# Expert results weighted before they are stored and added to their tokens' rows in DRAM: a routed expert stage on one Trainium2 core

## The chip, the cores and the metric

The kernel runs on 1 core of one Trainium2 chip. The metric is device time in microseconds (us) of one execution; the figure before the change is the median of three runs. Engines are named as in the profile: PE (TensorE), PEld (its weight loads), DVE (VectorE), ACT (ScalarE), POOL (GpSimd), SP (SyncE, which here only issues transfers). "DMA engines" are the core's 16 transfer engines, which all queues share.

## The reference, cut to what matters

Two transformer-like blocks run over 512 tokens of 1024 features (`S`, `D`), all in float32. The change touches the end of the second block: a mixture of experts, the residual sum and the last norm.

```python
hn2 = _rmsnorm(h, norm2_g) * (1.0 + scale2) + shift2
h = h + gate2 * _hier_moe(hn2, ...)
return _rmsnorm(h, final_g)
```

`_hier_moe` picks for each token one group of four (`MOE_GROUPS`) and in it the two best of eight experts (`EXPERT_TOPK`), each with a weight. An expert is silu(x Wgate) * (x Wup), times Wdown, with a hidden width of 256. So the 32 experts share 1024 (token, expert) results, and a token has exactly two, both in one group. The weights of all 32 experts are 96 matrices of 1 MiB each.

## The kernel before, in words

**Stages.** The program is a row of blocks; all engines meet between two of them. The first block of the reference, and the mixers of the second, are split float32 products (L210 to L212). The stage that matters is `nsa_end` (L2858): output projections, router, and then, in the same block, the experts, whose instruction streams `moe` (L3197) returns as five functions. `combine` (L3489) follows as a block of its own. A further pass over the experts (`moe_rest`, L3594) runs only if an expert has more than 64 tokens; the profile has no instruction of it.

**Experts in pairs.** Pair `i` of 16 (`NP_`) has experts `2i` and `2i+1`. Each gets 64 slots (`SLOTS`), so that a pair fills 128 partitions. `spread_ids` (L3447, DVE, 8 instructions), `find_ids` (L3455, PE) and `place_ids` (L3462, DVE) work out for every slot of a pair which token it holds: `from_row` is the token's row (0 to 511), `to_row` its result's row (the token's first or second expert: row t or 512 + t of `results`). An empty slot has an index beyond the bounds, and its row is not moved.

**A pair's work.** POOL gathers the tokens' rows from `rows` in DRAM (`gather`, L3471). PE turns them (L3233), DVE and ACT apply gain and shift (L3369, L3344), PE multiplies with the gate and up weights (L3257), ACT takes the silu (L3327), DVE the product (L3378), PE turns it (L3275) and multiplies with the down weights (L3288); DVE multiplies by the row of `gate2` into `y` (L3404, `take`), and POOL scatters the rows of `y` into `results` (L3438). `y` has four places; nothing orders one scatter behind the other.

**Weights.** 48 steps (`STEPS`, L1372), each one kind of matrix for both experts of a pair, 2 MiB in two DMAs of SP (`issue_step`, L1455), stand in this order: gate 0, up 0, then gate i, up i, down i-1. They have 8 places (`PLACES`). Steps 0 to 7 are issued as their places come free before and during the routing; step n of the others waits until PE is done with step n - 8 (L3220).

**The token rows.** After the last projection PE turns x into rows (`turn`, L2948), ACT scales them by the tokens' norm factor (`keep`, L3025) and SP stores them, four DMAs of 512 KiB, between steps 6 and 7 (L2918 to L2923). POOL waits for all four and for the pair's indices before it gathers pair 0 (L3189).

**The end.** `results` was filled with finite numbers during the attention (L2689). In `moe`, PE turns x once more (`turn_x`, L3239) and ACT keeps it (L3335). DVE works out each token's two weights (`shares`, L3381). When all scatters have landed, SP loads the first tile's two sets of results (L3222 to L3224), the block ends, `combine` loads the other three (L3502), DVE makes `x + w0 * first + w1 * second` (L3522, L3524) and the norm (L3528 to L3532, with ACT's L3514 and L3516), and SP stores each tile (L3506).

The order of SP's queue around the routing, as the code has it:

```python
                sp.wait_ge(logits_done, 1)
                self.issue_step(sp, 6)
                for t in range(TB):
                    sp.wait_ge(kept, t + 1)
                    sp.dma_start(d["rows"][toks(t), :], self.h_tok[:, t, :]).then_inc(rows_stored, 16)
                self.issue_step(sp, 7)
                moe_sync(sp)
```

## Time and profile before

| what | us |
|---|---|
| median of 3 runs | 2683.36 |
| lowest and highest of them | 2681.14, 2684.74 |
| the profiled execution's own time | 2686.17 |
| its span in the trace | 2684.1 |

The profiled execution took 2.07 us more than its span, and 2.81 us more than the median. Times of trace rows are from the start of the span. The profile's first part gives busy time of each engine, its second the span in 40 slices with the granted TensorE clock and the DMA engines' busy share; then come queues, the chain of work that ended last, the costliest groups of instructions, and the DMA issues with the time to landing. Views of a stretch give the same for some microseconds. A DMA's row gives the time that the issue took on its engine, not the transfer's.

### The profile page before, as it was taken

The numbers are of one execution on the slowest core, as the hardware profiler recorded it, in microseconds if no ns is written. First come the engines' busy times: TensorE is split into PE (matmuls) and PEld (weight loads), VectorE is DVE, ScalarE is ACT, GpSimd is POOL, SyncE is SP. The second block draws the span as 40 slices with busy tenths as digits, with TensorE's granted clock in tenths as the row PEclk, the third lists the DMA queues.
The fourth block names the chain that finished last, engine by engine and source line by source line (L and its number), as shares of the span: only waits on it lengthen the run. The fifth ranks groups of instructions, "written<-read, shape, count | busy, mean of one in ns | idle before, by whom it ended". The sixth has DMA issues, their size and how long they took to land. (4 is left out here: it accounts for less than half of the span.)

```text
span 2684.1 us, 33667 instructions
## 1 busy us (share of the span) xinstructions
PE 2524.1 (94%) x13581; PEld 1987.0 (74%) x13581; DVE 1482.2 (55%) x2202; ACT 998.0 (37%) x1412; POOL 331.6 (12%) x187
## 2 busy tenths in 40 slices
PE   8999999999999999999999999998999798979874
PEld 6777788888887778888887887776778565856542
DVE  4564456544636536545545665675764886445313
ACT  4246533222333555322223333334522587321112
POOL 0000004531400000225522000001000000001110
PEclk9999999999999999999999999999998897989997
DMA  4221133443322211434442334444352001369996
GB/s 151 82 72 55 63 117 119 143 142 127 107 90 74 64 63 64 141 104 144 146 142 79 94 84 133 151 133 127 117 180 79 17 15 66 96 255 371 424 425 249
DMA packets 265027, 355.99 MB, mean 133 GB/s; under 512 B 33444, under 2 KB 238756, under 8 KB 252196
## 3 DMA queue, kind: packets, MB, share of 16 engines
q1 hardware_dynamic: 256452, 333.30, 36.7%
q0 software_dynamic: 8320, 20.46, 2.1%
q8 instruction: 110, 1.80, 0.3%
q14 instruction: 49, 0.40, 0.0%
q10 hardware_dynamic: 96, 0.02, 0.0%
HBM read 337.38 MB, written 24.19 MB: 135 GB/s over the span
## 5 line engine op out<-in xcount | busy, mean ns | idle before, releaser
L210 PE MATMUL ps<-h_hi,w_hi 128*128 128x512 f32 (+1 forms) x1736 | 697.8, 402 | 22.0 <-DVE room L879 4.4
L212 PE MATMUL ps<-h_hi,w_lo 128*128 128x512 f32 (+1 forms) x1736 | 680.0, 392 | 0.0
L211 PE MATMUL ps<-h_lo,w_hi 128*128 128x512 f32 (+1 forms) x1736 | 680.0, 392 | 0.0
L187 ACT ACTIVATE w_hi<-w_raw 128x2048 fp32r<-128x2048 f32 (+1 forms) x168 | 316.8, 1886 | 742.5 <-PE ps L212 728.2
L192 DVE TENSOR_TENSOR w_lo<-w_raw,w_hi 128x2048 fp32r<-128x2048 f32 (+1 forms) x168 | 396.8, 2362 | 173.1 <-ACT w_hi L187 173.0
L210 PEld LDWEIGHTS ps<-h_hi,w_hi 128*128 128x128 f32 (+1 forms) x1736 | 328.2, 189 | 102.3 <-issue 35.5
L212 PEld LDWEIGHTS ps<-h_hi,w_lo 128*128 128x128 f32 (+1 forms) x1736 | 327.7, 189 | 71.2
L211 PEld LDWEIGHTS ps<-h_lo,w_hi 128*128 128x128 f32 (+1 forms) x1736 | 328.3, 189 | 69.8 <-issue 4.1
L210 PE MATMUL ps<-merged_hi,w_hi 128*128 128x512 f32 x640 | 249.8, 390 | 0.0
L212 PE MATMUL ps<-merged_hi,w_lo 128*128 128x512 f32 x640 | 249.1, 389 | 0.0
L211 PE MATMUL ps<-merged_lo,w_hi 128*128 128x512 f32 x640 | 249.0, 389 | 0.0
L1343 POOL TENSOR_TENSOR room<-room,silu_c 128x2048 f32<-128x2048 f32 x24 | 119.9, 4995 | 939.5 <-DMA room<-in_w_ada 939.5
L1271 DVE TENSOR_TENSOR x<-x,ps 128x1024 f32<-128x1024 f32 x38 | 46.4, 1221 | 224.5 <-PE ps L212 224.5
L212 PEld LDWEIGHTS ps<-merged_hi,w_lo 128*128 128x128 f32 x640 | 120.1, 188 | 25.2
L211 PEld LDWEIGHTS ps<-merged_lo,w_hi 128*128 128x128 f32 x640 | 120.2, 188 | 24.8
L210 PEld LDWEIGHTS ps<-merged_hi,w_hi 128*128 128x128 f32 x640 | 120.2, 188 | 24.6
L1346 POOL TENSOR_TENSOR room<-room 128x1024 f32<-128x1024 f32 (+1 forms) x48 | 117.3, 2444 | 3.8
L1289 DVE TENSOR_TENSOR merged_lo<-room,merged_hi 128x1024 fp32r<-128x1024 f32 x32 | 116.3, 3633 | 0.0
L879 DVE SCALAR_TENSOR_TENSOR room<-ps,x_rs 128x512 f32<-128x512 f32 x58 | 40.1, 691 | 134.5 <-PE ps L212 127.6
L1285 DVE SCALAR_TENSOR_TENSOR room<-ps,room 128x1024 f32<-128x1024 f32 x32 | 39.2, 1224 | 73.5 <-PE ps L212 73.3
L2818 ACT ACTIVATE nsa_p<-nsa_p,nsa_mx 128x512 f32<-128x512 f32 (+3 forms) x128 | 70.8, 554 | 18.8 <-DVE nsa_mx L2769 17.2
L3327 ACT ACTIVATE moe_silu<-ps 128x256 f32<-128x256 f32 x16 | 6.1, 383 | 171.8 <-PE ps L3257 171.8
(488 smaller groups left out, 3553.1 us busy)
## 6 DMA issues: line engine op xcount, KB each, us to landing
w_raw<-in_w_in SPq DMA_DIRECT2D x268, 256.0 KB, 3.7
w_raw<-in_w_up SPq DMA_DIRECT2D x128, 256.0 KB, 3.5
w_raw<-in_w_down SPq DMA_DIRECT2D x128, 256.0 KB, 3.7
room<-in_w_ada SPq DMA_DIRECT2D x96, 256.0 KB, 6.0
expert_over_h<-in_w_exp_down SPq DMA_DIRECT2D x10, 1024.0 KB, 25.3
w_raw<-in_w_out SPq DMA_DIRECT2D x32, 256.0 KB, 3.4
ssd_e<-chunk_decays SPq DMA_DIRECT2D x32, 256.0 KB, 4.4
w_raw<-in_w_ssm_out SPq DMA_DIRECT2D x32, 256.0 KB, 3.6
```

Of the source, the lines that this page charges most:

```text
L187: act.activation(self.hi[:, q, :, 0:cols], raw[:, q, :, 0:cols], ACT.Copy).then_inc(self.hi_ready, 1)
L192: dve.tensor_tensor(self.lo[:, q, :, 0:cols], raw[:, q, :, 0:cols], self.hi[:, q, :, 0:cols].bitcast(F32), ALU.subtract).then_inc(self.lo_ ...
L210: pe.matmul(out, w[0], x[0], start=start, stop=False)
L211: pe.matmul(out, w[0], x[1], start=False, stop=False)
L212: return pe.matmul(out, w[1], x[0], start=False, stop=stop)
L879: dve.scalar_tensor_tensor(kept(t, c), bank(t, c), factor, x_rs[:], ALU.mult, ALU.mult).then_inc(taken0 if c == 0 and t != T_SWK else W.ev ...
L1271: dve.tensor_tensor(two(self.x, t), two(self.x, t), self.pst[:, q, 0:n, :], ALU.add).then_inc(W.evicted[q], 1)
L1285: dve.scalar_tensor_tensor(r[:, q], self.pst[:, q, 0:n, :], 0.0, rs.unsqueeze(1).to_broadcast([P, n, S]), ALU.max, ALU.mult).then_inc(W.ev ...
L1289: dve.tensor_tensor(two(u[1], t), r[:, q], two(u[0], t).bitcast(F32), ALU.subtract).then_inc(u_low, 1)
L1343: pool.tensor_tensor(w, w, c, ALU.mult).then_inc(ada_step, 1)
L1346: pool.tensor_tensor(w[:, 0:half], w[:, 0:half], w[:, half:2 * half], ALU.add).then_inc(ada_step, 1)
L2818: act.activation(p[:, i, e, 0:W], p[:, i, e, 0:W], ACT.Exp, bias=mx[:, i, e:e + 1], scale=-1.0, accum_out=den[:, i, e:e + 1]).then_inc(exp ...
```

## The change

Every result is multiplied by its token's weight when DVE takes it from PSUM (the third operand of `take`), so that a token's two results can simply be added. The scatter becomes an indirect DMA with `compute_op=ALU.add` into the token's own row of `results`, where x was stored beforehand. What it takes:

- **Pairs of two groups.** `expert_of(i, j)` pairs expert e of group 0 with expert e of group 1 (pairs 0 to 7), and of groups 2 and 3 (pairs 8 to 15). A token's experts lie in one group, so no token is twice in a pair.
- **Indices.** `place_ids` makes a third index, `add_row`: the token's row, or for an empty slot row 512 + p of partition p. All 128 rows of a pair are in bounds and are written. One more DVE instruction in front of `placed`, one behind it.
- **Adds one after the other.** POOL waits until scatter i - 1 has landed before it issues scatter i.
- **x in DRAM.** PE turns x a second time right behind the token rows (`turn(4)` to `turn(7)`), ACT copies it to `y` (`x_kept`), SP stores it to `results`, four DMAs of 512 KiB, once gathers 0 and 1 have landed. `take` of pairs 0 to 3 waits for these stores. The filling of `results` in the attention, `turn_x` and `take_x` are gone.
- **SP's order.** The token rows are stored ahead of step 6. Step 7 follows behind the stores of x.
- **Weights by slot.** `shares` moves from the sixth pair to the start; ACT stores the 2 x 512 weights (two DMAs from 128 partitions, 4 bytes a piece) to `d["shares"]` behind its first silu; POOL clears a small tile once and gathers, for each pair, 128 single weights by `to_row` (16 indirect DMAs more).
- **The wait for `passed`** moves from PE's first turn of `moe` to its first down product.
- **The end.** SP loads all four tiles of `results` in `moe` (four DMAs in place of eight in two blocks); `combine` has no adds, only the norm.

The diff, cut to what runs:


```diff
@@ -1389,6 +1389,11 @@
...
+def expert_of(i, j):
+
+    return (2 * (i // ME) + j) * ME + i % ME
+
...
@@ -1457,7 +1462,7 @@
...
+            w = self.d[("w_exp_gate_2", "w_exp_up_2", "w_exp_down_2")[kind]].rearrange("o e k n -> (o e) k n")[expert_of(i, e)]
...
@@ -2686,16 +2691,12 @@
...
-                for i in range(2):
-                    part = self.d["results"][i * S:(i + 1) * S, :].rearrange("(p r) n -> p (r n)", p=P)
-                    sp.dma_start(part, self.x[:].rearrange("p k s -> p (k s)")).then_inc(filled, 16)
...
-                sp.wait_ge(filled, 16 * 2)
...
@@ -2915,11 +2916,16 @@
                 W.done(sp, *wo[3])
                 for n in range(3, 6):
                     self.issue_step(sp, n)
-                sp.wait_ge(logits_done, 1)
-                self.issue_step(sp, 6)
                 for t in range(TB):
                     sp.wait_ge(kept, t + 1)
                     sp.dma_start(d["rows"][toks(t), :], self.h_tok[:, t, :]).then_inc(rows_stored, 16)
+                sp.wait_ge(logits_done, 1)
+                self.issue_step(sp, 6)
+                for i in range(2):
+                    sp.wait_ge(self.x_landed[i], 16)
+                for t in range(TB):
+                    sp.wait_ge(x_kept, t + 1)
+                    sp.dma_start(d["results"][toks(t), :], self.y[:, t]).then_inc(x_stored, 16)
                 self.issue_step(sp, 7)
                 moe_sync(sp)
 
@@ -2946,10 +2952,12 @@
...
-                    if t >= 2:
+                    if 2 <= t < TB + 2:
                         pe.wait_ge(kept, t - 1)
+                    elif t >= TB + 2:
+                        pe.wait_ge(x_kept, t - TB - 1)
                     for k in range(KC):
-                        mm = pe.transpose(turn_ps(t)[:, k * P:(k + 1) * P], self.x[:, k, toks(t)], self.c("ident"))
+                        mm = pe.transpose(turn_ps(t)[:, k * P:(k + 1) * P], self.x[:, k, toks(t % TB)], self.c("ident"))
...
@@ -3000,9 +3008,8 @@
...
-                for t in range(1, TB):
+                for t in range(1, 2 * TB):
                     turn(t)
-                pe.wait_ge(kept, TB)
...
@@ -3010,14 +3017,15 @@
...
+                pe.wait_ge(x_kept, TB)
...
+                pe.matmul(self.ps[:, 5, 0:1], self.c("ones"), over[:], start=True, stop=True).then_inc(over_sum, 1)
                 pe.wait_ge(gate_taken, 1)
-                pe.matmul(self.ps[:, 1, 0:1], self.c("ones"), over[:], start=True, stop=True).then_inc(over_sum, 1)
...
@@ -3064,6 +3072,9 @@
...
+                for t in range(TB):
+                    act.wait_ge(turned, TB + t + 1)
+                    act.activation(self.y[:, t], turn_ps(TB + t), ACT.Copy).then_inc(x_kept, 1)
...
@@ -3112,7 +3123,7 @@
...
+                link(dve.tensor_scalar(self.id_work[:, 4:5], self.c("token1")[:, 0:1], float(S - 1), None, ALU.add))
...
@@ -3221,7 +3233,8 @@
...
-            self.load_results(sp, 0, self.results_landed)
+            for t in range(TB):
+                sp.dma_start(self.first[:, t], d["results"][t * P:t * P + P, :]).then_inc(self.results_landed[t], 16)
...
@@ -3280,6 +3282,8 @@
...
+                else:
+                    pe.wait_ge(passed, 1)
...
-            pe.wait_ge(passed, 1)
...
@@ -3347,6 +3339,10 @@
...
+            act.wait_ge(shared, 1)
+            for i in range(2):
+                to = d["shares"][i * S:(i + 1) * S, :].rearrange("(t p) o -> p (t o)", p=P)
+                act.dma_start(to, self.place_w[:, i], allow_slow_non_contiguous=True).then_inc(shares_stored, 16)
...
@@ -3401,10 +3395,14 @@
...
-                dve.tensor_tensor(y[:, i % YR], y_ps, self.gate_row, ALU.mult).then_inc(y_ready, 1)
+                else:
+                    dve.wait_ge(x_stored, 16 * TB)
+                dve.wait_ge(self.share_landed[i % 4], self.shares_before + 16 * (i // 4 + 1))
+                dve.scalar_tensor_tensor(y[:, i % YR], y_ps, share[:, i:i + 1], self.gate_row, ALU.mult, ALU.mult).then_inc(y_ready, 1)
...
+            shares()
...
@@ -3429,14 +3425,27 @@
...
+            def gather_share(i):
+                pool.indirect_dma_start(share[:, i:i + 1], None, d["shares"], bass.IndirectOffsetOnAxis(ap=self.to_row[:, i:i + 1], axis=0),
+                                        bounds_check=2 * S - 1, oob_is_err=False).then_inc(self.share_landed[i % 4], 16)
+
+            pool.memset(share[:], 0.0).then_inc(share_cleared, 1)
             gather(2)
             gather(3)
+            pool.wait_ge(share_cleared, 1)
+            pool.wait_ge(shares_stored, 32)
+            for i in range(4):
+                gather_share(i)
             for i in range(NP_):
                 if i + 4 < NP_:
                     gather(i + 4)
                 pool.wait_ge(y_ready, i + 1)
-                pool.indirect_dma_start(d["results"], bass.IndirectOffsetOnAxis(ap=self.to_row[:, i:i + 1], axis=0), y[:, i % YR], None,
-                                        bounds_check=2 * S - 1, oob_is_err=False).then_inc(y_stored[i % YR], 16)
+                if i >= 1:
+                    pool.wait_ge(y_stored[(i - 1) % YR], 16 * ((i - 1) // YR + 1))
+                pool.indirect_dma_start(d["results"], bass.IndirectOffsetOnAxis(ap=self.add_row[:, i:i + 1], axis=0), y[:, i % YR], None,
+                                        bounds_check=2 * S - 1, oob_is_err=True, compute_op=ALU.add).then_inc(y_stored[i % YR], 16)
+                if i + 4 < NP_:
+                    gather_share(i + 4)
...
@@ -3460,23 +3469,19 @@
...
         link(dve.scalar_tensor_tensor(to, v, -1.0, none, ALU.add, ALU.add))
         dve.tensor_copy(self.to_row[:, i:i + 1], to)
         link(dve.tensor_scalar(back, to, float(S), -float(S), ALU.is_ge, ALU.mult))
-        dve.tensor_tensor(self.from_row[:, i:i + 1], to, back, ALU.add).then_inc(placed, 1)
+        link(dve.tensor_tensor(token, to, back, ALU.add))
+        dve.tensor_copy(self.from_row[:, i:i + 1], token).then_inc(placed, 1)
+        dve.tensor_tensor(self.add_row[:, i:i + 1], token, spare, ALU.min)
...
@@ -3490,17 +3495,14 @@
...
-                for t in range(1, TB):
-                    self.load_results(sp, t, landed)
...
-                    act.wait_ge(summed, t + 1)
+                    act.wait_ge(landed[t], 16)
...
-                def add(t):
-                    dve.wait_ge(landed[t], 32)
-                    dve.scalar_tensor_tensor(first[:, t], first[:, t], self.place_w[:, 0, t:t + 1], x_tok[:, t], ALU.mult, ALU.add).then_inc(weighted, 1)
-                    dve.wait_ge(weighted, t + 1)
-                    dve.scalar_tensor_tensor(first[:, t], second[:, t], self.place_w[:, 1, t:t + 1], first[:, t], ALU.mult, ALU.add).then_inc(summed, 1)
-
                 def norm(t):
...
-                add(0)
-                for t in range(1, TB):
-                    add(t)
-                    norm(t - 1)
-                norm(TB - 1)
+                for t in range(TB):
```

## Rows read from the trace of the kernel before

**Rows 1.** The page: span, then DMA share and rate in 40 slices.

```profile
span 2684.1 us, 33667 instructions
...
DMA  4221133443322211434442334444352001369996
```

**Rows 2.** Two stretches: PE, PEld, DVE, ACT, POOL busy, clock, DMA share, GB/s.

```profile
2406.00:2408.00 2.00, 0.00 (x0) 0.00 (x0) 0.45 (x2) 0.00 (x0) 0.09 (x1) 0.50 0.98 410
...
2410.00:2412.00 2.00, 0.00 (x0) 0.00 (x0) 0.00 (x0) 0.00 (x0) 0.35 (x1) 0.50 0.51 142
```

**Rows 3.** Stretches of the expert stage, the same columns.

```profile
2440.00:2500.00 60.00, 60.00 (x465) 36.83 (x466) 38.16 (x158) 11.36 (x30) 10.11 (x10) 1.00 1.01 422
2500.00:2560.00 60.00, 51.81 (x376) 29.81 (x372) 14.73 (x37) 9.08 (x24) 8.07 (x8) 0.97 1.01 424
2560.00:2620.00 60.00, 47.11 (x332) 26.52 (x334) 11.03 (x23) 7.80 (x21) 6.03 (x6) 0.97 1.01 425
...
2640.00:2645.00 5.00, 4.22 (x22) 1.46 (x21) 0.28 (x1) 1.02 (x1) 0.00 (x0) 1.00 0.38 162
```

**Rows 4.** Order of time around the routing: start, length, engine, line, idle before it.

```profile
2385.17 3.73 SPq L2922 DMA_DIRECT2D token_rows<-nsa_gate  x4
...
2388.94 2.14 SPq L1461 DMA_DIRECT2D expert_over_h<-in_w_exp_down  x2
...
2403.47 0.16 DVE L3469 TENSOR_TENSOR from_row<-id_work 128x1 int32<-128x1 f32 x1
...
2407.91 1.13 POOL L3472 DMA_INDIRECT nsa_gate<-token_rows,from_row  x1 [331.38 <-DMA token_rows<-nsa_gate]
...
2412.30 1.95 PE L3233 MATMUL ps<-const,nsa_gate 128*128 128x128 f32 x8 [7.83 <-DMA nsa_gate<-token_rows,from_row]
...
2415.88 5.74 PE L3257 MATMUL ps<-expert_first,moe_x 128*64 128x256 f32 x32 [1.64 <-issue]
...
2421.65 0.80 SPq L1461 DMA_DIRECT2D expert_first<-in_w_exp_gate  x2
...
2423.22 1.50 ACT L3344 ACTIVATE moe_x<-ps,par 128x128 f32<-128x128 f32 x4 [1.18 <-PE ps L3233]
...
2427.25 3.67 PE L3257 MATMUL ps<-expert_over_w,moe_x 128*64 128x256 f32 x32
```

**Rows 5.** DMA queues and issues, 2340 to 2684 us; last column: issue to landing.

```profile
q0 software_dynamic: 4608, 8.40, 6.5%
...
nsa_gate<-token_rows,from_row POOLq DMA_INDIRECT x16, 10.3
token_results<-results,to_row POOLq DMA_INDIRECT x16, 8.3
```

**Rows 6.** Order of time at the end of the stage.

```profile
2646.72 0.97 POOL L3438 DMA_INDIRECT token_results<-results,to_row  x1 [14.39 <-DVE results L3404]
...
2651.78 0.97 POOL L3438 DMA_INDIRECT token_results<-results,to_row  x1 [4.09 <-DVE results L3404]
...
2655.47 0.43 SPq L3479 DMA_DIRECT2D w_raw<-token_results  x1
2659.13 1.28 ACT L3511 ACT_TABLE_LOAD   x1 [7.31 <-PEq L2862]
...
2677.64 1.04 ACT L3514 ACTIVATE fin_sq<-expert_first 128x1024 f32<-128x1024 f32 x1
...
2677.97 1.28 DVE L3532 SCALAR_TENSOR_TENSOR w_raw<-expert_first,fin_rs,ps 128x1024 f32<-128x1024 f32 x1
...
2679.78 1.28 DVE L3532 SCALAR_TENSOR_TENSOR w_raw<-expert_first,fin_rs,ps 128x1024 f32<-128x1024 f32 x1
```

**Rows 7.** The two stores of gains, 1024 pieces of 4 bytes each.

```profile
L2693 SPq DMA_DIRECT2D row_gains<-par x2: 1107/5320/9534, 2212.6 to 2213.8; - x2
...
DMA to landing us min/median/max: 17.0/17.5/18.0
```

**Rows 8.** Last scatter alone: its DMA issue and landing.

```profile
token_results<-results,to_row POOLq DMA_INDIRECT x1, 3.2
```

More of the change, by code:

```diff
@@ L2677, in nsa_attention @@
             o_parts = self.h
[L2678 removed]
+            gains_stored, gains_landed = sem("gains_stored"), sem("gains_landed")
             block = st.enter_context(nc.Block())
@@ L3180, in _ @@
                 dve.wait_ge(chosen, 2)
-                dve.tensor_tensor(self.over[:], self.over[:], self.comb[:], ALU.mult)
+                link(dve.tensor_tensor(self.over[:], self.over[:], self.comb[:], ALU.mult))
                 dve.wait_ge(over_sum, 1)
-                dve.tensor_scalar(self.passes[:], self.ps[:, 1, 0:1], 1.0, None, ALU.min).then_inc(passed, 1)
+                dve.tensor_scalar(self.passes[:], self.ps[:, 5, 0:1], 1.0, None, ALU.min).then_inc(passed, 1)
                 moe_vector(dve)
@@ L3210, in moe @@
         far, part = sb("moe_far", [P, TB, NE]), sb("moe_part", [P, TB, NE])
+        share = sb("moe_share", [P, NP_])
         y = self.y
@@ L3236, in turn @@
                 t.then_inc(x_turned_high, 1)
-            def turn_x(t):
-                if t == 0:
-                    pe.wait_ge(xg_ready, NP_)
-                    pe.wait_ge(xg_ready_high, NP_)
-                else:
-                    pe.wait_ge(tok_taken, t)
-                for k in range(KC):
-                    e = pe.transpose(x_ps[:, k * P:(k + 1) * P], self.x[:, k, t * P:(t + 1) * P], self.c("ident"))
-                e.then_inc(tok_turned, 1)
             def hidden(i, kind, out, done):
@@ L3333, in take_hidden @@
                 act.activation(uT[:, i % 2], u_ps.rearrange("p (k s) -> p k s", k=2), ACT.Copy).then_inc(u_ready, 1)
-            def take_x(t):
-                act.wait_ge(tok_turned, t + 1)
-                act.activation(rows[:, t, :], x_ps, ACT.Copy).then_inc(tok_taken, 1)
             def take_rows(i):
@@ L3420, in vector @@
                     take_rows(i + 2)
-                if 2 * i + 4 == NP_:
-                    shares()
             take(NP_ - 1)
@@ L3462, in place_ids @@
     def place_ids(self, dve, i, src, link, placed):
-        none, to, back = (self.id_work[:, j:j + 1] for j in range(3))
+        none, to, back, token, spare = (self.id_work[:, j:j + 1] for j in range(5))
         v = src[:, 2 * i:2 * i + 1]
@@ L3473, in gather @@
                                 bounds_check=S - 1, oob_is_err=False).then_inc(self.x_landed[i % TB], 16)
-    def load_results(self, sp, t, landed):
-        for i, to in enumerate((self.first, self.second)):
-            sp.dma_start(to[:, t], self.d["results"][i * S + t * P:i * S + t * P + P, :]).then_inc(landed[t], 16)
     def gain_row(self, pe):
@@ L3492, in combine @@
             sem, clear = self.stages.open("combine", st)
-            weighted, summed, squared, mean, root, inverse, made, out_done = (sem(x) for x in (
-                "weighted", "summed", "squared", "mean", "root", "inverse", "made", "out_done"))
+            squared, mean, root, inverse, made, out_done = (sem(x) for x in ("squared", "mean", "root", "inverse", "made", "out_done"))
             sb = lambda nm, s: st.enter_context(nc.sbuf_tensor(nm, s, F32))
             sq, rs = sb("fin_sq", [P, 2, D]), sb("fin_rs", [P, TB])
-            first, second, x_tok, landed = self.first, self.second, self.h_tok, self.results_landed
+            first, second, landed = self.first, self.second, self.results_landed
             block = st.enter_context(nc.Block())
@@ L3557, in _ @@
             def _(sp):
-                sp.wait_ge(self.results_landed[0], 32)
+                for t in range(TB):
+                    sp.wait_ge(self.results_landed[t], 16)
                 sp.wait_ge(low, KC)
@@ L3724, in renew @@
             turned, taken = sem("turned"), sem("taken")
-            landed = [sem("landed")]
             block = st.enter_context(nc.Block())
-            @block.sync
-            def _(sp):
-                self.load_results(sp, 0, landed)
-                sp.wait_ge(landed[0], 32)
             @block.tensor
@@ L3741, in _ @@
                 self.gain_row(pe)
-            @block.scalar
-            def _(act):
+            @block.vector
+            def _(dve):
                 for t in range(TB):
-                    act.wait_ge(turned, t + 1)
-                    act.activation(self.h_tok[:, t], self.flat(0, D), ACT.Copy).then_inc(taken, 1)
+                    dve.wait_ge(turned, t + 1)
+                    dve.tensor_tensor(self.first[:, t], self.first[:, t], self.flat(0, D), ALU.add).then_inc(taken, 1)
             @block.gpsimd
```

37 lines of the change are left out of this document (15 added, 22 removed).

## The prediction, made before the changed kernel was run

> **What bounds the kernel now.** I read the page first: PE is the busiest engine over the span, but the DMA slices are at 9 tenths from about 2415 us on [rows 1], which is the expert stage alone. So I asked for stretches of that stage. From 2440 to 2620 us the DMA engines are busy all the time at 422 to 425 GB/s, while PE falls from fully busy (60.00 of 60 us) to 47.11 of 60 [rows 3]. PE sets the pace only until its backlog of loads is used up; the end of the stage is set by the bytes that the 16 DMA engines have to move. A step of 2 MiB (2.10 MB) costs 4.95 us at 424 GB/s, and what else passes through these engines is added to the end.
>
> The order of time around the routing [rows 4] shows how the stream begins: the token rows are stored from 2385.17, POOL's first gather starts only at 2407.91 because it waits for them, PE turns that gather's rows at 2412.30, and the first gate product (2415.88, 5.74 us) frees the place for step 8 at 2421.65. The DMA engines were out of work by about 2411 (share 0.98, then 0.51) [rows 2]: some 11 us of hole that nothing fills. After the last weights comes a tail in which hardly anything runs beside anything else [rows 6]: the last scatter is issued at 2651.78 and lands 3.2 us later [rows 8], at 2654.98; SP loads, the block changes, ACT loads its table at 2659.13, the last product of the norm starts at 2679.78, and the span ends at 2684.1, 29.1 us behind the landing.
>
> So three places count: the start of the stream, its volume, and the tail. The filling of results in the attention (4.2 MB) was not under a DMA limit; removing it gains nothing.
>
> **The start.** SP's queue is served in order, so the row stores now stand behind steps 3 to 5 and no longer behind step 6. That takes 4.95 us off their landing, so gather 0 may start at 2407.91 - 4.95 = 2403.0. Pair 1's indices are ready at 2403.63 [rows 4], plus its 0.16, plus 0.2 for the added DVE step of the same size, plus some 0.6 to POOL: gather 1 at 2404.6. The first gather before took 4.4 us to PE's turn (2407.91 to 2412.30); now it shares the engines with step 6, and a gather under load takes up to 10.3 (median) [rows 5]. I take 4.6 us of gain for turn and gate: step 8 is issued at about 2417. But SP holds the x stores and step 7 until both gathers have landed, at about 2410. The engines, which would have ended at 2411 with step 7, end at 2406 without it, and start again at 2410.8. Then come x (2.10 MB, 4.95 us) and step 7 (4.95 us), to 2420.7, where step 8 already waits. Before, step 8's bytes began at about 2422.4. The stream is therefore **1.7 us** earlier; bounds: 0 (gathers delayed as under load) to 5 (gathers at once).
>
> Work hidden there: four more turns on PE (8 transposes each; such a turn took 1.95 us at 2412.30 [rows 4]) and four copies on ACT lie beside DVE's chain of routing steps, on which PE waits for the chosen experts anyway. Without that cover they would cost up to 4 x 1.95 = 7.8 us. The weights' sums on DVE fall into its wait for the first gate product (5.74 us).
>
> **Weights by slot.** ACT issues two DMAs of 512 pieces of 4 bytes behind its first silu, in front of its half of pair 1's rows (2423.22, 1.50 us, done at 2424.72; PE's gate 1 starts at 2427.25 [rows 4], so 2.5 us are to spare). The nearest rows are SP's stores of 1024 such pieces: 1.1 us to issue the first, 9.5 us the second behind a full ring, 17 to 18 us to landing behind a backlog [rows 7]. ACT's ring is empty; I take 2 x 1.1 us, hidden. The upper end, 2 x 9.5, would hold gate 1 for 16 us, of which the x stores and step 7 as backlog cover 4; 12 us would remain. POOL's 16 more gathers carry 4 bytes a row; with the stores I take **1.0 us** of DMA time for all of them (ends: 0, and 16 x 0.70 = 11 if they cost what a scatter of rows costs).
>
> **The volume.** A scatter before moved the filled slots alone: 1024 rows in 16, so 64 rows or 0.262 MB each, 0.62 us at 424 GB/s (by the queue: 6.5% of 344 us for 32 transfers, 0.70 us [rows 5]). Now all 128 rows are in bounds: 0.524 MB, 1.24 us if only writing counts. An add also reads its row of results. The trace has no add; its nearest rows are a scatter, which writes a row, and a gather, which reads one. Lower end: the read costs nothing, 1.24 us. Upper end: write, read and source each take their turn, 3.71 us. I take write plus read, **2.47 us**, because in this stage the engines have no idle share in which a read could hide [rows 3]. Fourteen scatters (0 to 13) lie in front of the last weights' landing: 14 x (2.47 - 0.62) = **+25.9 us**; ends +8.7 and +43.3.
>
> The Trainium skill, "Collectives: The Full Stack", section on the bandwidth ceiling, says that an add in the DMA needs two reads for one write and so runs at about half a copy's rate. By it the term would be the 2.47 us that I took; no row of this trace shows it. The same page, at its stop on SDMA and CCE, calls the add itself free.
>
> **The waits between adds.** A pair's bytes take 3 x 4.95 + 2 x 0.62 = 16.1 us now; a scatter lands in 8.3 us (median) under load [rows 5], an add by the same reading in 10 to 12, so the wait for scatter i - 1 is over before scatter i is ready, except at the end. There scatter 14 goes at 2646.72 and 15 at 2651.78, 5.06 apart. Alone, a scatter landed in 3.2 us with 0.62 of transfer, so an add takes 2.6 + 2.5 = 5.1: 14 lands at 2651.8, POOL goes 0.8 later (2652.6), and 15 lands at 2657.7, **2.7 us** later than 2654.98 (all on top of the shift of the stream).
>
> **The tail.** From the last landing S: ACT's table load started at S + 4.15. SP issues four loads instead of two in front of the block's end, 0.43 each: S + 5.0. Table 1.28, then 1.8 for the square and the small steps before the product (2.14 from the last square's start at 2677.64 to its product's, some of it a wait; the square alone is 1.04 [rows 6]): S + 8.1. Then a product of 1.28 for each tile, one every 1.81 us (2677.97 to 2679.78, the last two, which have no adds between them [rows 6]): the last ends at S + 8.1 + 3 x 1.81 + 1.28 = S + 14.8. From there to the end 3.0 as now: S + 17.8 against S + 29.1. Gain 11.3, less 2.7: **-8.6 us**. Four loads of 1.24 us each land in time for it.
>
> **Sum.** -1.7 + 1.0 + 25.9 - 8.6 = +16.6 us. The profiled execution's own time is 2686.17: 2702.8. It stood 2.8 above the median 2683.36, to which the same sum gives **2700.0 us**.
>
> **Rivals.**
>
> *The add costs no more than its write (faster or the same).* Then +8.7 in place of +25.9; scatter 14 lands in time (2.6 + 1.24 = 3.8) and S moves by 0.6: tail -10.7. Sum -1.7 + 1.0 + 8.7 - 10.7 = -2.7, 2680.7. It may be better still: while 2640 to 2645 the mean DMA share is 0.38 [rows 3], so some engines lag, having had more filled slots. If the laggards wrote full shares already, the empty slots' rows load only the others, and the term falls to about 0: 2672. It decides for "faster" where a scatter costs less than 0.4 us over today's. For it: reads and writes are different directions of an engine. Against: the source is read as well, so the reading side alone has twice the bytes. Chance 0.28.
>
> *Adds much dearer, or in each other's way.* If an add takes three row times (3.71 us), the term is +43.3, S moves by 5 and the tail is -6: 2683.4 - 1.7 + 1.0 + 43.3 - 6 = 2720. It also holds from the point where an add under load lands later than the pairs' 16 us; the wait for the one before then makes POOL, and through the four places of y DVE, the pace. For: no row bounds an add's latency. Against: twice the median landing would be needed. Chance 0.15.
>
> *The start does not come forward*, because the gathers run into step 6 or the weights' stores hold up ACT, or the stores are not ordered as said: 2700 + 1.7 to + 14. Chance 0.05 by itself.
>
> My forecast: 0.52. Its own range, from the start's bounds and the laggards, is 2692 to 2706. Since both signs hold much of the chance, the whole range reaches from the first rival's better half, 2675, to the second's 2720.
>
> About 0.2% of this kernel (5.4 us) can be told from no change. Faster by more: 0.18 (some six tenths of the first rival). Same: 0.17 (the rest of it, and the forecast's cheap end with a late pair of bounds). Slower: 0.65.
>
> **What would show it.** Right: DMA share near 1 from 2411 to the last weights; the last weights landing some 25 us later; the queue of the indirect DMAs with about four times a scatter's share; step 8 issued at about 2417 and not the start of its bytes; last landing to end 18 us. Wrong: the last weights at 2650 or earlier (the read is free), POOL waiting on a scatter's landing in mid-stage (adds collide), PE's second gate product waiting on ACT (the weights' stores).

## The result, and the profile after: slower, by two to two and a half times what was forecast

| what | us |
|---|---|
| changed kernel, median of 5 runs | 2725.98 (four of them 2722.95 to 2727.24) |
| kernel before beside it, median of 5 | 2684.74 (2681.14 to 2687.68) |
| ratio, with its 95% interval | 1.0147 (1.0134 to 1.016) |
| forecast, with its range | 2700.0 (2675 to 2720) |
| the changed kernel again, in a second comparison, median of 4 | 2719.53 (2717.09 to 2720.97) |
| ratio there | 1.0134 (1.0113 to 1.0155) |

The change costs 41 us in the first comparison and 34 in the second; the forecast was +16.6 and its range ended at +37. The sign was right and the size was not. Measured against the kernel itself the loss is small, 1.3 to 1.5%, but both intervals lie clear of 1. The one profiled execution of the first comparison took 8796 us, over three times the others, so all rows below come from the profiled execution of the second one: span 2716.8 us, 32.7 above the 2684.1 of before.

**The end of the stage, the changed kernel (order of time: start, length, engine, line, idle before it).**

```profile
2685.40 1.56 POOL L3445 DMA_INDIRECT token_results<-results,add_row  x1 [15.95 <-DVE results L3401]
...
2692.47 1.55 POOL L3445 DMA_INDIRECT token_results<-results,add_row  x1 [5.51 <-DMA token_results<-results,add_row]
2698.60 1.75 SPq L3237 DMA_DIRECT2D expert_first<-token_results  x4
2703.94 1.28 ACT L3513 ACT_TABLE_LOAD   x1 [19.79 <-PEq L2863]
...
2712.48 1.28 DVE L3528 SCALAR_TENSOR_TENSOR w_raw<-expert_first,fin_rs,ps 128x1024 f32<-128x1024 f32 x1
```

Scatter 14 is issued 38.7 us later than before (2646.72 [rows 6]). From there the end is 6.0 us shorter: 31.4 us to the span's end, against 37.4. So 38.7 - 6.0 = 32.7 is the whole difference. The tail gave something back; the loss lies in front of scatter 14.

**Where in the stage, the changed kernel (stretches: PE, PEld, DVE, ACT, POOL busy, clock, DMA share, GB/s).**

```profile
2406.00:2408.00 2.00, 1.11 (x6) 1.14 (x7) 0.00 (x0) 0.00 (x0) 0.00 (x0) 0.50 0.22 84
...
2410.00:2412.00 2.00, 1.52 (x8) 1.07 (x10) 0.72 (x3) 1.66 (x3) 0.00 (x0) 0.50 1.04 424
...
2420.00:2460.00 40.00, 21.68 (x152) 12.92 (x148) 11.71 (x53) 3.04 (x8) 6.96 (x7) 0.78 1.00 328
2460.00:2480.00 20.00, 18.96 (x129) 12.07 (x131) 12.09 (x58) 3.77 (x10) 6.36 (x6) 0.84 0.80 272
...
2500.00:2560.00 60.00, 53.01 (x393) 31.53 (x391) 23.17 (x87) 9.08 (x24) 15.20 (x13) 0.97 1.02 387
2560.00:2620.00 60.00, 45.99 (x302) 24.96 (x300) 10.59 (x22) 9.02 (x24) 13.85 (x12) 0.89 1.02 396
```

Read the last two columns. From 2500 us the engines are as full as before and move 387 to 396 GB/s where they moved 424 to 425 [rows 3]: dearer bytes beside the weights, as forecast. From 2420 to 2460 the share is also 1.00, but the rate is 328 GB/s, and PE is busy for half the stretch. From 2460 to 2480 the share itself falls to 0.80. Nothing in the forecast accounts for these sixty microseconds.

**Who waits there (engine, line, what for: us in total, times, longest), 2410 to 2480 us, the changed kernel.**

```profile
POOL moe_share L3429 <- DMA result_shares<-place_weight: 26.4, 1, 26.4
...
DVE results L3401 <- DMA moe_share<-result_shares,to_row: 18.8, 1, 18.8
...
PE ps L3467 <- DVE moe_ids L3460: 15.5, 1, 15.5
```

**The same in order of time.**

```profile
2416.46 1.08 ACTq L3345 DMA_DIRECT2D result_shares<-place_weight  x2
...
2445.19 1.06 SPq L1466 DMA_DIRECT2D expert_over_m<-in_w_exp_down  x2
...
2451.30 1.00 POOL L3429 DMA_INDIRECT moe_share<-result_shares,to_row  x1 [26.41 <-DMA result_shares<-place_weight]
...
2468.74 0.80 SPq L1466 DMA_DIRECT2D expert_over_h<-in_w_exp_gate  x2
```

This is a chain. ACT issues the two stores of weights at 2416.46, in 1.08 us, exactly as cheap as forecast. One lands 19.9 us behind its issue and the other 33.6 (the next view has the median, 26.7). POOL needs both: it has waited since 2424.9, which makes 26.4 us, when it gathers the first weights at 2451.30. DVE waits 18.8 us for a gathered weight in the take of pair 0, and everything queued behind that take waits too: the ids of the next pair (`moe_ids`), for which PE waits 15.5 us, and with PE the release of weight places. SP issues no step between 2445.19 and 2468.74, and the stream runs dry.

**DMA issues with their KB and the median time to landing, 2340 to 2717 us, the changed kernel.**

```profile
q0 software_dynamic: 5120, 12.60, 15.0%
q10 hardware_dynamic: 1056, 0.00, 0.2%
...
nsa_gate<-token_rows,from_row POOLq DMA_INDIRECT x16, 11.1
moe_share<-result_shares,to_row POOLq DMA_INDIRECT x16, 8.9
token_results<-results,add_row POOLq DMA_INDIRECT x16, 10.4
result_shares<-place_weight ACTq DMA_DIRECT2D x2, 2.0 KB, 26.7
```

An add lands in 10.4 us (median) against 8.3 of a plain scatter [rows 5], and the queue of the indirect DMAs (q0) takes 15.0% of 377 us, 56.5 us, where it took 6.5% of 344, 22.4 us.

### The profile page after: what moved, and what is told of

Read it like the earlier page. It is cut to its first block and busy times, and to the rows that moved or that the text cites. A ratio compares the mean times of both kernels' runs of the same rounds, so it can differ in the third digit from the quotient of the medians.

```text
span 8794.6 us, 33743 instructions
## 1 busy us (share of the span) xinstructions
PE 8729.3 (99%) x13581; PEld 4581.8 (52%) x13581; DVE 1388.8 (16%) x2227; ACT 1010.4 (11%) x1412; POOL 278.1 (3%) x204
## 5 line engine op out<-in xcount | busy, mean ns | idle before, releaser
L210 PE MATMUL ps<-h_hi,w_hi 128*128 128x512 f32 (+1 forms) x1736 | 1951.4, 1124 | 15.8 <-DVE room L879 3.5
L211 PE MATMUL ps<-h_lo,w_hi 128*128 128x512 f32 (+1 forms) x1736 | 1901.4, 1095 | 0.0
L212 PE MATMUL ps<-h_hi,w_lo 128*128 128x512 f32 (+1 forms) x1736 | 1892.8, 1090 | 0.0
L210 PEld LDWEIGHTS ps<-h_hi,w_hi 128*128 128x128 f32 (+1 forms) x1736 | 743.5, 428 | 718.9 <-issue 715.8
L211 PEld LDWEIGHTS ps<-h_lo,w_hi 128*128 128x128 f32 (+1 forms) x1736 | 760.1, 438 | 653.1 <-issue 653.1
L212 PEld LDWEIGHTS ps<-h_hi,w_lo 128*128 128x128 f32 (+1 forms) x1736 | 733.3, 422 | 668.9 <-issue 665.6
L210 PE MATMUL ps<-merged_hi,w_hi 128*128 128x512 f32 x640 | 703.9, 1100 | 0.0
L211 PE MATMUL ps<-merged_lo,w_hi 128*128 128x512 f32 x640 | 702.7, 1098 | 0.0
L212 PE MATMUL ps<-merged_hi,w_lo 128*128 128x512 f32 x640 | 695.1, 1086 | 0.0
L211 PEld LDWEIGHTS ps<-merged_lo,w_hi 128*128 128x128 f32 x640 | 280.4, 438 | 246.1 <-issue 246.1
```

Of the source, the lines that this page charges most:

```text
L210: pe.matmul(out, w[0], x[0], start=start, stop=False)
L211: pe.matmul(out, w[0], x[1], start=False, stop=False)
L212: return pe.matmul(out, w[1], x[0], start=False, stop=stop)
```

## The experiments

Twelve runs. "Stage" is a length that doesn't depend on when an execution reached the experts (that moves by up to 10 us between profiled executions): from the first store of token rows to the issue of scatter 14, both read from the order of time of each trace. It comes from one trace of each run, and differences of stages are taken before they are rounded. "Over before" is the median less that of the kernel before in the same comparison (2685.80, 2686.71 or 2685.62 us). The labels that begin with b or c start from the kernel before, the others from the changed one.

| run | what is different | stage, us | over before, us | ratio, 95% |
|---|---|---|---|---|
| kernel before | | 261.6 | | |
| e1_again | nothing | 301.8 | +33.7 | 1.0134 (1.0113 to 1.0155) |
| e2_write_all | no add: rows written | 284.6 | +13.9 | 1.0056 (1.0034 to 1.0078) |
| e3_add_filled | empty slots not moved | 294.1 | +26.7 | 1.0098 (1.0074 to 1.0123) |
| e4_write_filled | both | 278.0 | +7.4 | 1.0031 (1.0016 to 1.0045) |
| e5_no_weights | no weights by slot | 290.1 | +17.3 | 1.0061 (1.0044 to 1.0078) |
| e6_turned_weights | weights stored from 8 rows | 287.7 | +19.2 | 1.0069 (1.0052 to 1.0085) |
| e8_old_order | rows behind step 6 again | 304.5 | +36.8 | 1.0136 (1.0119 to 1.0152) |
| b1_rows_first | only SP's order | 260.9 | -2.0 | 0.9995 (0.9985 to 1.0004) |
| e9_pieces16 | weights' pieces 16 bytes | 287.4 | +21.1 | 1.0083 (1.0067 to 1.0098) |
| e11_turned_write_filled | e6 and e4 | 264.7 | -5.2 | 0.9978 (0.9969 to 0.9987) |
| b2_rows_loads | order, all loads at once | 260.8 | +1.3 | 1.0001 (0.9992 to 1.001) |
| c2_rows_hold_loads | b2, step 7 held | 258.2 | -1.2 | 0.9991 (0.9982 to 1.0) |

### The changed kernel again, and its scatter taken apart

e1_again has no edit. e2 leaves out the sum (a token's row holds its last result):

```diff
-    bounds_check=2 * S - 1, oob_is_err=True, compute_op=ALU.add).then_inc(y_stored[i % YR], 16)
+    bounds_check=2 * S - 1, oob_is_err=True).then_inc(y_stored[i % YR], 16)
```

e3 indexes the add by `from_row`, so that empty slots lie beyond the bounds; e4 does the same without the add (it leaves the sum out as well):

```diff
-    bass.IndirectOffsetOnAxis(ap=self.add_row[:, i:i + 1], axis=0) ... bounds_check=2 * S - 1, oob_is_err=True
+    bass.IndirectOffsetOnAxis(ap=self.from_row[:, i:i + 1], axis=0) ... bounds_check=S - 1, oob_is_err=False
```

> The changed kernel once more, unchanged, for a trace at the usual TensorE pace (the profiled execution of the first run took 8796 us with matmuls three times as long). Theory A (the adds): the 14 adds in front of the last weights cost more than the 2.47 us predicted for each; an add row took 328 ns on a DMA engine against 159 ns for a plain row, and a whole add 3.4 us of 16 engines' time against 0.7 us, so the last weights should land some 14 x 2.7 = 38 us later than before, less 2. Theory B (the waits): the adds cost about the 25 us predicted, and the rest of the 41 us lies in PE or DVE waiting (for weights by slot, for x, for the add before), seen as holes in the DMA share between 2420 and the last weights. Expected by A: DMA share 1.0 all through; by B: below 0.95 in stretches.

> The changed kernel with the add left out: the same 128 rows a pair are written plainly over the tokens' rows (so the sums are left out of the result). Everything else stays, the wait for the scatter before too. Theory A: a scatter then costs 8 x 0.159 = 1.3 us in place of 3.4, so 14 x 2.1 = 30 us less in the stream and 2 to 4 us less at the end: 2690 to 2697 us. Theory B: 14 x 1.24 = 17 us less at most, since the waits stay: 2703 to 2712 us.

> The changed kernel with adds for the filled slots only (empty slots out of bounds, rows not moved): half the rows. Theory A with cost per row: 14 x 1.5 = 20 us less and 2 to 3 less at the end, 2700 to 2706 us. Theory A with a fixed stall per add rather than a cost per row: only some 10 us less, 2712 to 2717. Theory B: 12 us less.

> Neither the add nor the empty slots: filled rows written plainly over the tokens' rows (sums left out of the result). The DMA volume of the scatters is then that of the kernel before, and what is left of the change is the start, the weights by slot, the wait between scatters and the shorter end. My sum without the volume term: 2683.4 - 1.7 + 1.0 - 11.3 = 2671 to 2673 us. Theory B: the waits remain, 2680 us or more.

Queue of the indirect DMAs, 2340 to 2717 us, first e2, then e4 (packets, MB, share of 16 engines):

```profile
q0 software_dynamic: 5120, 12.60, 8.8%
```

```profile
q0 software_dynamic: 5120, 8.41, 6.3%
```

Of 377 us these are 33.2 and 23.8 us, and the changed kernel's 15.0% is 56.5. So in the queue the read of an add costs (56.5 - 33.2) / 16 = 1.46 us per scatter, and the rows of empty slots (33.2 - 23.8) / 16 = 0.59. With all rows in bounds the stage says nearly the same: 301.8 - 284.6 = 17.1 us for fourteen reads, 1.22 each; 284.6 - 278.0 = 6.7 for the empty rows. The read is not hidden: the rival by which an add costs only its write falls, and so does the one by which it costs three row times.

e3 does not fit this count by rows. Its line of the same view:

```profile
q0 software_dynamic: 5120, 8.41, 9.6%
```

That is 36.2 us of queue time. So in the queue an add of the filled rows alone costs 12.4 us more than a write of them (e4), about half of the 23.3 us that it costs for all rows. In the stage it costs 294.1 - 278.0 = 16.1 us, almost the 17.1 of all rows, and taking the empty rows out of the adds gives back only 7.7 us where it frees 20.3 in the queue. The medians agree: the add costs 19.3 us with filled rows and 19.8 with all. What e3's time fits is the expectation of a fixed price for each add (2712 to 2717 us). There is another reading, the laggards of the prediction: if the engines that carry most filled slots set when the last weights land, empty rows load only the others. The mean share of the 16 engines over the last 20 us of the stage is 0.30 in e3 and 0.67 in the changed kernel, so in e3 most of them have run dry while the last weights are awaited. No view shows single engines, and no run separates the two. (e2's 2699.7 us lies between its two expectations: 19.8 us less, where the second gave 17 at most.)

Still, e4, whose scatter moves what the old one moved, has a stage 16.4 us longer than before. The volume explains only 23.8 of 40.2 us.

### The weights by slot

e5 takes out the stores and gathers of weights, and the results stay unweighted:

```diff
-            act.wait_ge(shared, 1)
-            for i in range(2):
-                to = d["shares"][i * S:(i + 1) * S, :].rearrange("(t p) o -> p (t o)", p=P)
-                act.dma_start(to, self.place_w[:, i], allow_slow_non_contiguous=True).then_inc(shares_stored, 16)
...
-            pool.wait_ge(shares_stored, 32)
-            for i in range(4):
-                gather_share(i)
...
-                if i + 4 < NP_:
-                    gather_share(i + 4)
```

> The changed kernel without the weights by slot: no stores of them, no 16 gathers, and the results are added unweighted (the weighting is left out of the result). In the trace of the changed kernel the two stores of 512 pieces of 4 bytes took about 27 us to land, POOL waited 26.4 us for them, DVE 18.8, the DMA engines moved only some 300 to 340 GB/s at a busy share of 1.0 from 2415 to 2460, and from 2460 to 2480 the share fell to 0.80. Theory W (weights): some 10 us of lost rate and 4 us of hole go, 2703 to 2707 us. Rival (the rate is lost to x stores and gathers in that stretch): 2715 or more.

e6 keeps everything, but PE turns the 128 x 8 weights behind its first gate product, ACT copies them, and one DMA stores eight rows of 512 bytes:

```diff
+            pe.transpose(share_ps, self.place_w[:].rearrange("p i t -> p (i t)"), self.c("ident")).then_inc(shared, 1)
...
-            for i in range(2):
-                to = d["shares"][i * S:(i + 1) * S, :].rearrange("(t p) o -> p (t o)", p=P)
-                act.dma_start(to, self.place_w[:, i], allow_slow_non_contiguous=True).then_inc(shares_stored, 16)
+            act.activation(share_rows[:], share_ps, ACT.Copy).then_inc(shared, 1)
+            act.wait_ge(shared, 3)
+            act.dma_start(d["shares"].rearrange("(r p) o -> r (p o)", p=P), share_rows[:]).then_inc(shares_stored, 16)
```

> The changed kernel with the weights turned on PE first (one transpose, one copy on ACT), so that one DMA of 8 pieces of 512 bytes stores them; the 16 gathers stay. Nothing is left out. Theory W with the 4-byte writes as the cause: as without weights, 2703 to 2708 us. If the gathers of single weights or anything on ACT's queue cost as much, it stays at 2715 to 2720.

e9 stores the same 4 KB from the same 128 partitions, but so that a partition's four values of each store lie side by side in DRAM: 256 pieces of 16 bytes in place of 1024 of 4. The weights then reach the wrong slots:

```diff
-                to = d["shares"][i * S:(i + 1) * S, :].rearrange("(t p) o -> p (t o)", p=P)
+                to = d["shares"][i * S:(i + 1) * S, :].rearrange("(p t) o -> p (t o)", p=P)
```

> The changed kernel with the same two stores of weights, but each partition's four weights as one piece of 16 bytes (256 pieces in place of 1024; the weights then stand in another order in DRAM, so the results are weighted wrongly, with the same work). If the stall goes with the number of pieces: a quarter of the 13.7 us that turning the weights won back stays, 2708 to 2711 us, landing 8 to 12 us instead of 27. If it is a fixed delay of a second queue's DMA behind the weights' stream: 2716 to 2720, landing above 20 us.

The stretches of e6 that answer to the changed kernel's (same columns), and e9's landing and wait:

```profile
2420.00:2460.00 40.00, 39.21 (x310) 25.44 (x311) 26.83 (x124) 8.53 (x24) 14.39 (x13) 1.00 1.02 400
2460.00:2480.00 20.00, 20.00 (x148) 11.31 (x146) 11.68 (x48) 2.27 (x6) 3.68 (x4) 1.00 1.03 375
```

```profile
result_shares<-place_weight ACTq DMA_DIRECT2D x2, 2.0 KB, 8.5
```

```profile
POOL moe_share L3429 <- DMA result_shares<-place_weight: 2.8, 1, 2.8
```

e5, e6 and e9 shorten the stage by 11.7, 14.1 and 14.4 us. (Why e5, which does least, gains least is open; its median is the lowest of the three.) What the three have in common is that the 1024 pieces of 4 bytes are gone. e6 and e9 keep all sixteen gathers of weights, so the gathers are not the cost, and e9 keeps the queue, the issuing engine, the partitions and the bytes, so it is the number or the size of the pieces; e9 changes both. e9's two stores land in 7.1 and 10.0 us (median 8.5) in place of 19.9 and 33.6, and POOL's wait of 26.4 us becomes 2.8. e9 was to keep a quarter of the loss, if that went with the number of pieces; it keeps none that these runs can see.

The loss has two parts. In e6 (which reached the stage 3.5 us later) the engines moved 40 x 400 = 16.0 MB from 2420 to 2460 us, in the changed kernel 13.1 MB: 2.9 MB, or 6.8 us at 424 GB/s. From 2460 to 2480 it is 7.5 against 5.4 MB: 4.9 us more. Together these are 11.7 of the 14.1 us. The second part is the hole that the late weights tore. The first is stranger, as the engines' share was full. The DMA queues of 2420 to 2455 us, the changed kernel, then e6 (packets, MB, share):

```profile
DMA packets 2790, 11.02 MB, mean 315 GB/s; under 512 B 1388, under 2 KB 1388, under 8 KB 1504
q1 hardware_dynamic: 1444, 10.52, 93.5%
q10 hardware_dynamic: 1056, 0.00, 1.7%
```

```profile
q1 hardware_dynamic: 1688, 12.27, 84.9%
q10 hardware_dynamic: 16, 0.00, 0.1%
```

The tiny pieces' own packets (q10) take 1.7% of the engines' time. It is the weights' packets (q1) beside them that take longer: 93.5% of the time for 10.52 MB, 8.9% a MB, where e6 has 6.9% a MB. The adds have no part in it: e4, which has the 4-byte pieces and no adds, moves 330 GB/s from 2420 to 2460 us. So the price of such a store does not stand in its own queue's row. The Trainium skill, "DMA: Bandwidth & Descriptors", section Specifications, puts the smallest transfer for full rate at 512 bytes and says that shorter ones are done by read, modify and write. That 1024 pieces of 4 bytes were dear agrees. But e9's 256 pieces of 16 bytes are below 512 as well and cost next to nothing, so being shorter than 512 bytes was not enough here.

### The order of SP's queue, and the loads of the end

e8 puts the token rows behind step 6 again in the changed kernel. b1 makes the reverse move in the kernel before, where it is the whole edit:

```diff
-                sp.wait_ge(logits_done, 1)
-                self.issue_step(sp, 6)
                 for t in range(TB):
                     sp.wait_ge(kept, t + 1)
                     sp.dma_start(d["rows"][toks(t), :], self.h_tok[:, t, :]).then_inc(rows_stored, 16)
+                sp.wait_ge(logits_done, 1)
+                self.issue_step(sp, 6)
```

> The changed kernel with the token rows stored behind step 6 again, as before the change. If the early rows are worth what I predicted (the first gather 5 us earlier, hence x stores, step 7 and all that follows): 2724 us, 4 to 5 more. If the start is hidden behind the stall for the weights: no difference, 2718 to 2721.

> The kernel before with one thing of the change: token rows stored ahead of step 6, with step 7 right behind step 6. The 11 us hole in front of step 8 should shrink by the 4.95 us that the rows come earlier: 2680 to 2681 us, if gather and gate follow. If the gathers are slowed by step 6 and 7 in flight (a gather under load lands in 7 to 10 us, not 4): 2683 to 2686.

The start of b1 (order of time):

```profile
2403.03 1.14 POOL L3472 DMA_INDIRECT nsa_gate<-token_rows,from_row  x1 [325.85 <-DMA token_rows<-nsa_gate]
...
2410.89 1.95 PE L3233 MATMUL ps<-const,nsa_gate 128*128 128x128 f32 x8 [6.68 <-DMA nsa_gate<-token_rows,from_row]
```

The gather goes 4.9 us earlier, as forecast (4.5 if counted from the first row store), but PE's turn follows 7.9 us behind it, against 4.4 in the kernel before: it now runs beside steps 6 and 7. Step 8 is issued at 2420.29 against 2421.65, and the stage is 0.7 us shorter. In the changed kernel step 7 is held behind the gathers, and the turn comes 4.7 us after the first gather (2402.18 to 2406.89); there the old order costs 2.7 us of stage, while the ratios of e8 and e1 cannot be told apart. b1's time is that of its second expectation, gathers slowed by the steps in flight.

b2 adds to b1 that SP issues all eight loads of results in `moe`; c2 adds to b2 that step 7 waits for gathers 0 and 1:

```diff
+                for i in range(2):
+                    sp.wait_ge(self.x_landed[i], 16)
                 self.issue_step(sp, 7)
...
-            self.load_results(sp, 0, self.results_landed)
+            for t in range(TB):
+                self.load_results(sp, t, self.results_landed)
```

> The kernel before with the token rows ahead of step 6 and all eight loads of results issued in moe, before the block ends, as the change does with its four. The loads of tiles 1 to 3 are then issued at 2656 and not at 2659.5, and DVE's adds and norms (4.3 us a tile) follow at once after the block's change: 3 to 4 us less at the end, 2679 to 2682 us. If DVE's chain of four tiles sets the end and the loads were hidden: 2683 to 2686.

> As the last, and step 7 held until gathers 0 and 1 have landed, as the change has it (without its stores of x). The gather for pair 0 took 7.9 us to PE's turn with step 7 in flight and 4.4 without. Held: gate 0 done 3 to 4 us earlier, step 7 lands in time: 2676 to 2679 us. If the gathers are slowed by step 6 anyway: as the last, 2680 to 2682.

c2's stage is 3.4 us shorter than the kernel before's, and still its time is not. The loads gave it back: from the first load's issue to the end c2 takes 32.5 us, the kernel before 29.0. In b2 DVE's first add starts 11.4 us behind the first load's issue, against 7.8, and the chain of four tiles hangs on the first. It does not wait for data: the first tile's two loads land 3.6 and 4.5 us behind their issues in b2, and 3.7 and 4.6 in the kernel before.

```profile
2659.33 0.33 SPq L3480 DMA_DIRECT2D expert_first<-token_results  x1
...
2670.72 1.28 DVE L3521 SCALAR_TENSOR_TENSOR expert_first<-expert_first,place_weight,nsa_gate 128x1024 f32<-128x1024 f32 x1 [15.48 <-issue]
```

"Issue" is a wait for nothing that the profile names. What does move is a handful of packets of the kind "instruction" (queues q8 and q14, 5 packets, 49 KB): in the kernel before they run 4.7 us behind the first load, in b2 there is none until 8.3 us behind it, while q1 is full, and the first add follows 1.5 to 2 us behind the last of them in both. So the eight loads seem to have held up the loading of the next block's instructions; no run takes that apart. Both runs missed their expectations of a gain (2679 to 2682 and 2676 to 2679 us).

### Both causes removed

> All of the change but its volume and its 4-byte pieces: turned weights, filled slots only, written without the add (the sums are left out of the result). If the account closes: 2693.2 less the 13.7 us of the weights, 2679 to 2681 us, against my sum without the volume of 2671 to 2673; the rest, some 8 us, would be the start (predicted 1.7 early) and what is left of the weights by slot. If turning the weights only helped because adds ran beside them: 2688 or more.

e11 is e6's store of weights with e4's plain scatter of the filled rows (it leaves the sums out). Its stage is 264.7 us. With e6 and e1 this gives a full account of the stage: 261.6 before; **+3.1** for all the rest of the change (e11, whose 2680.4 us lie in the expected 2679 to 2681); **+23.0** for the add and the empty rows (e6 less e11); **+14.1** for the 4-byte pieces (e1 less e6); 301.8 in sum. The parts are worth much the same in the other order (23.8 for the volume beside the pieces, 13.3 for the pieces without it). Without both causes the remainder is 5.2 us faster than the kernel before, by ratio 0.9978 (0.9969 to 0.9987). No version that keeps the whole computation was faster than the kernel before by more than 0.2%.

## Why the prediction was wrong, step by step

**What bounds the kernel: right.** The stage is bound by the DMA engines' bytes, and what was taken out of that volume (e2, e3, e4) came out of the stage's length, though not always in proportion.

**Weights by slot: the step that failed.** "I take 2 x 1.1 us, hidden", and 1.0 us of DMA time for stores and gathers. The issue did take 1.08 us, and ACT held up nobody: PE's first up product ran at 2417.90 at once behind its turn, and the second gate product at 2422.04 at once behind PE's next step. The 1024 pieces cost 14.1 us all the same. I priced the issue and the engine that issues, and the bytes, but not what the row I used said last: 17 to 18 us from issue to landing [rows 7]. I wrote that off as a backlog. POOL's gathers wait for that landing, DVE for the gathers, PE for DVE. By that row alone the stores land at 2416.5 + 17.5 = 2434, and a gather under load is 10.3 us more [rows 5]: 2444, while the take of pair 0 ran at 2439.80 in the kernel before. Some 4 us of wait were there to be read. The loss of rate beside the pieces, 6.8 us, and with it the later landing, could not be read from any row of before: those stores ran where the DMA engines had time to spare.

**The volume: the sum right, 25.9 forecast and 23.0 to 23.8 measured; its rule only in the queue.** With all rows in bounds the reads came to 17.1 us for 14 x 1.24 = 17.4 forecast, the empty rows to 6.7 for 8.7. But the same rule gives 8.7 us for adding the filled rows alone in place of writing them, and the stages of e3 and e4 give 16.1. So the agreement of the 17.1 is in part luck: what an add costs this stage did not go with its rows, and whether a fixed price or the fullest engines make it stays open. Indirect scatters take about four times the old one's queue time: (56.5 - 16 x 0.70) / 16 = 2.8 us against 0.70, with the weights' gathers in it. The page "Collectives: The Full Stack" of the Trainium skill, section on the bandwidth ceiling, says that an add runs at about half a copy's rate, two reads for one write. The queue's time agrees: less 0.70 us each for the gathers of rows, an add takes 2.8 us against 1.4 for a write of all rows, and 1.6 against 0.8 for the filled rows. Whether the adding itself costs something these runs cannot tell: the 1.46 us of queue time for the read lie 0.22 above the 1.24 of its bytes.

**The start: right in kind, and a loss at the end of the stage that the forecast did not have.** Step 8 was forecast for 2417 and was issued at 2416.45; counted from the first row store it came 3.7 us earlier than before (32.8 against 36.5), for 4.6 forecast. (The working adds the 0.16 us of pair 1's last index step twice, which changes little.) The x stores (4.95 us of engine time) were to fall into the hole; the hole was there (share 0.22 from 2406 to 2408) and the engines were full from 2410. Start and weights' gathers together were to give -1.7 + 1.0 = -0.7, and e11's stage is 3.1 us longer. But the start is not where that was lost. From 240 us into the stage to scatter 14, the queue of weights and x (q1) had 5.2 MB left to move in e11 (95.70 less 90.49) and 6.0 in the kernel before (93.90 less 87.88), so e11 was 0.8 MB or 1.9 us ahead, as "1.7 us earlier" has it; the same count gives 3.6 us for c2, whose stage is 3.4 us shorter. The loss lies behind that: over the last 20 us of the stage the engines' mean share is 0.43 in e11 and 0.68 before, and the last down product ahead of scatter 14, which waits for its weights, starts 258.9 us into the stage in place of 255.9. The forecast had no term for when the last weights land once most engines are done. Pairs of other experts, the weights' gathers and POOL's wait for each scatter are all in e11; which of them makes it was not separated.

**The waits between adds: right in kind.** In mid-stage POOL never waited for an add. At the end it did, 5.51 us. Scatter 15 goes 7.07 us behind 14 (5.06 before), and the first load 6.13 us behind scatter 15 (3.32 before): 4.8 us lost for the 2.7 forecast. An add alone takes 5.9 to 6.2 us to land, not 5.1, and its issue holds POOL for 1.56 us, where a plain scatter's took 0.97.

**The tail: right.** From the first load's issue to the end it is 18.2 us, and was 29.0: a gain of 10.8 where 11.3 was forecast. Less the 4.8 above, the end gave 6.0 for 8.6.

**Sum in this execution:** stage +40.2 (forecast 25.2), end -6.0 (forecast -8.6), first row store 1.5 us earlier: +32.7. The forecast lacked 16.1 us: 14.1 for the 4-byte pieces, 3.8 in what e11 keeps (-0.7 forecast, +3.1 measured), 2.6 at the end, less 2.9 of volume and the 1.5. Why the first comparison found 41 us and the second 34 stays open; an execution's earlier stages move by several microseconds, and nothing in the runs separates that.

## What to carry to other kernels

Read a store's time to landing, not its issue, whenever something waits for it, and don't put a thousand 4-byte pieces beside a saturated stream: turn the few values on PE first or lay them side by side, which here gave back 14 us for one transpose. An add in the DMA took twice a write's time in its queue, and an index that is in bounds for an empty slot is paid too (6.7 to 7.7 us of stage here). A sum of engine time is not the length of a stage: ask also which engine finishes last; in this stage, which is bound by bytes, two loads and an addition at the end were cheaper. Moving a transfer forward in a queue moves only the issue: ask what it then runs beside.

## What the runs showed of the hardware that was not expected

- 1024 pieces of 4 bytes (4 KB in two stores) took 19.9 and 33.6 us to land beside the weights; 256 pieces of 16 bytes took 7.1 and 10.0. From 2420 to 2455 us the 4-byte pieces' own packets took 1.7% of the engines' time, but each MB of the weights beside them took 8.9% where it takes 6.9% otherwise, so the engines read as full (1.00) at 328 GB/s.
- An indirect DMA with an add holds POOL for 1.56 us against 0.97 to 1.0 for a plain one of the same shape (e2), and lands 10.4 us (median) behind its issue under load and in 5.9 to 6.2 alone; e2's plain ones land in 8.6 and 3.3.
- Halving the rows of the adds halved their extra time in the queue (23.3 to 12.4 us) and hardly changed their extra cost to the stage (17.1 to 16.1 us).
- With eight loads issued ahead of the block's change in place of two (b2), that block's first DVE instruction came 3.6 us later, though its own data had landed no later.
- The same gather of 128 rows took 4.4 us to PE's turn with the stream running out, and 7.9 beside two weight steps.
